# Positive scores in a queue of SBUF buffers, and value low parts on GpSimd from f32 copies

## The chip, the core and the metric

The kernel is written in Bass for one core of a Trainium2 chip. A core has a matrix engine (TensorE, PE in the profile; PEld its weight loads), three elementwise engines (VectorE = DVE, ScalarE = ACT, GpSimd = POOL), a sequencer that mainly issues transfers (SyncE = SP), an on-chip memory of 128 partitions (SBUF) and an accumulator memory of eight banks of 512 f32 columns (PSUM). Each engine runs its own queue in order; engines meet at semaphores that instructions count up and waits test. The metric is the device time of one execution in microseconds.

## What is computed

A trunk of two layers over 1024 tokens of width 1024. Layer 0 is stick-breaking and forgetting attention, layer 1 a sparse attention: an indexer scores all keys with 16 small heads, each query keeps its 256 best visible keys, and 16 heads attend over one shared latent. Each layer has a gated feed-forward with a causal convolution. The part of the reference that the change touches:

```python
idx_logits = jax.nn.relu(jnp.einsum('bqhd,bsd->bqhs', qib, kif))
score = jnp.einsum('bqh,bqhs->bqs', wb, idx_logits) * IDX_SCALE
score = jnp.where(visible[None], score, -jnp.inf)
top_val, top_idx = lax.top_k(score, topk)          # topk = 256
...
p = jax.nn.softmax(jnp.where(valid, logits, -jnp.inf), axis=-1)
ctx = einsum('bqhk,bqkc->bqhc', p, k_sel[..., DSA_ROPE:])
o = jnp.einsum('bshc,hcd->bshd', ctx, w_uv)        # per head; the kernel projects the latent first: values
```

## The kernel before, in words

Matrices are multiplied as bf16 pairs: every operand is split into a high part (the value cast to bf16) and a low part (the value minus its high part), and a product is three matmuls (high by high, low by high, high by low). The program is a list of phases. Each phase has a program for each engine, and an engine goes from one phase to the next with no barrier, held by semaphores alone.

**The index phase** (`index_sync`, `index_gpsimd`, `index_tensor`, `index_scalar`, `index_vector`). Eight strips `s` of index queries, two heads each. TensorE projects strip `s` in eight units of six matmuls (`strip_unit`, L1739) and, between the units, computes scores of strip `s - 2`: 12 score steps, one for each of two heads and six query blocks of 384 to 1024 columns (`scores`, L1783). Step t of a strip; a global number g counts them all. Step g writes the PSUM bank pair 0-1 or 2-3 in turn. ScalarE takes the relu of the pair in place (`relu`, L1837), VectorE multiplies it by the head's weight and adds it to `score` in SBUF (`add`, L1896; the first six, L1893, only multiply), and TensorE's step g waits for add g - 2 (the semaphore `s_ia`). The steps of strips 6 and 7 run beside two strips of the next product (`feed_q`).

For each strip ScalarE also copies the projection out of PSUM (`copy_strip`, L1811) and issues four DMAs that swap rows for the rotary embedding (L1816); GpSimd multiplies the swapped copy by the sine table (L1757) and splits one piece of weights (`split_piece`: `w_hi` L262, `w_lo` L265); VectorE multiplies by the cosine (L1865), adds the two (`rotate`, L1871) and later writes the low parts of the queries (`lows`, L1903), after ScalarE's high parts (`highs`, L1845). The order on ScalarE is: copy and DMAs of strip s, relus 0 to 4 of strip s - 1, highs of strip s, relus 5 to 11. On VectorE: cosine of s, adds 0 to 2, rotate, adds 3 to 6, lows, adds 7 to 11.

**The top-k phase** (`topk_*`). VectorE runs 32 rounds of `max` (L2106) and `match_replace` (L2110) over the six score blocks, then writes the additive mask `hide` (L2115 and small fills), and then the low parts of the attention values (`val_lo`, L2127). Meanwhile TensorE projects the 32 strips of queries (L292), ScalarE copies them out and makes high parts, GpSimd rotates and makes low parts (`q_out`, L2082). At its end TensorE projects the values in 16 chunks of 512 columns, one bank each (L2009): six matmuls a chunk. ScalarE writes the high part of a chunk (L2059), VectorE the low part from PSUM and the high part. Chunks 8 to 15 reuse banks and wait for `s_vl`, the count of low parts.

**Attention** (`attend_*`). TensorE waits for 12 low parts and computes the first latent scores (L2192), VectorE adds `hide` and takes the row maximum (L2270), ScalarE the exp (L2251), TensorE turns the result (L2228), and the product with the values follows (L2207). GpSimd copies the current heads' values (`v_now`, L2316) once all 16 low parts are there.

Elsewhere in the kernel VectorE normalises rows with L1255, a `scalar_tensor_tensor` whose two tensor operands are both in SBUF, while GpSimd splits weights.

## Time and profile before

| | us |
|---|---|
| median of 3 runs | 2972.35 (2971.84 to 2978.59) |
| profiled execution, device time | 2972.27 |
| its span in the trace | 2970.5 |
| PE busy | 2815.2 (95%) |
| DVE busy | 1890.6 (64%) |
| POOL busy | 1627.0 (55%) |
| ACT busy | 1082.4 (36%) |

In the trace the score steps run from about 1363 us of the span to 1546, the top-k rounds from there to 1877, the second half of the value chunks from 1883 to 1897, and attention from then on.

In a row of a timeline the first number is the start in microseconds of the span, the second the duration; a bracket at the end gives how long the engine stood idle before it and which instruction released it. Instructions of one engine overlap a little in these records, so the step from one start to the next is shorter than the duration (by about 0.08 us on VectorE). Matmul records are pipelined: what counts is the distance between their starts. A tile's name has its buffer number left out: `ps` is all of PSUM.

### The profile page before, as it was taken

To read this page: it belongs to the slowest core of one execution; us is meant where nothing else is said; L and a number is where in the kernel's file an instruction comes from. 1 tells how busy PE (TensorE), PEld (TensorE's weight loads), DVE (VectorE), ACT (ScalarE), POOL (GpSimd) and SP (SyncE) were. 2 spreads that over 40 slices of the span, in tenths; PEclk is the share of its full clock that TensorE was granted. 3 is DMA by queue.
4 is the path that set the end of the run, shared out by engine and by line. 5 is a ranking of instruction groups with operands and counts; after the bars stand their busy time and mean duration, and the time that the engine had idled before them with its cause. 6 is when DMAs were issued, how large, how long until landed. Compare 5 with 4: busy or idle time off the path is not lost.

```text
span 2970.5 us, 44602 instructions
## 1 busy us (share of the span) xinstructions
PE 2815.2 (95%) x16880; PEld 1459.1 (49%) x16880; DVE 1890.6 (64%) x2795; ACT 1082.4 (36%) x1781; POOL 1627.0 (55%) x867
## 2 busy tenths in 40 slices
PE   7999998899999999998789999799999999999998
PEld 3566655444444444443334444477764444444443
DVE  5777566485666674155679999777765856665042
ACT  3566676324333310014454333466650433332000
POOL 4777321456766778844238777300007566775884
PEclk9999999999999999999999999899999999999999
DMA  4122221431111143222103222111113211112422
GB/s 143 51 64 61 69 68 32 156 114 57 57 57 57 64 170 121 101 81 67 47 28 141 107 81 89 57 58 56 42 43 121 106 55 59 57 57 99 142 100 99
DMA packets 102988, 240.56 MB, mean 81 GB/s; under 512 B 42448, under 2 KB 42576, under 8 KB 102848
## 3 DMA queue, kind: packets, MB, share of 16 engines
q1 hardware_dynamic: 56352, 204.13, 19.2%
q10 hardware_dynamic: 46496, 34.48, 4.5%
q8 instruction: 97, 1.59, 0.2%
q14 instruction: 43, 0.35, 0.0%
HBM read 185.31 MB, written 31.51 MB: 73 GB/s over the span
## 4 chain that ended last, share of the span: by engine, by line
PE 70%; DVE 17%; issue 4%; ACT 4%; POOL 2%; ACTq 2%; DMA 0%; DVEq 0%; POOLq 0%
PE ps L1413 22%; PE ps L303 17%; PE ps L2192 6%; DVE best L2106 5%; DVE score L2110 5%; PE ps L553 5%; PE ps L327 4%; PE ps L292 3%; PE ps L2228 2%; PE ps L663 2%; PE ps L559 2%; PE ps L748 2%; PE ps L1739 1%; PE ps L2207 1%; PE ps L725 1%
## 5 line engine op out<-in xcount | busy, mean ns | idle before, releaser
L262 POOL TENSOR_TENSOR w_hi<-w_stage,ones 128x1024 bf16<-128x1024 f32 x147 | 303.9, 2067 | 342.7 <-PE ps L303 231.5
L265 POOL TENSOR_TENSOR w_lo<-w_stage,w_hi 128x1024 bf16<-128x1024 f32 x147 | 337.2, 2294 | 11.5
L1240 DVE SCALAR_TENSOR_TENSOR x_res<-x_res,ps 128x1024 f32<-128x1024 f32 x32 | 39.0, 1217 | 344.1 <-PE ps L303 344.1
L303 PE MATMUL ps<-w_hi,hid_hi 128*128 128x512 bf16 x704 | 209.6, 379 | 5.0 <-DVE x_res L1240 4.1
L303 PE MATMUL ps<-w_hi,hid_lo 128*128 128x512 bf16 x704 | 209.5, 379 | 0.0
L303 PE MATMUL ps<-w_lo,hid_hi 128*128 128x512 bf16 x704 | 209.4, 379 | 0.0
L2192 PE MATMUL ps<-lat_hi,q_now 128*128 128x512 bf16 (+3 forms) x768 | 197.7, 326 | 0.0
L1202 ACT ACTIVATE ln_rstd<-ln_rstd 128x1 f32<-128x1 f32 x32 | 6.5, 203 | 517.7 <-DVE ln_rstd L1249 517.7
L292 PE MATMUL ps<-xt_hi,w_hi 128*128 128x512 bf16 x608 | 180.9, 379 | 2.4 <-DVE score L1896 2.4
L292 PE MATMUL ps<-xt_lo,w_hi 128*128 128x512 bf16 x608 | 181.0, 379 | 0.0
L292 PE MATMUL ps<-xt_hi,w_lo 128*128 128x512 bf16 x608 | 180.9, 379 | 0.0
L2316 POOL COPY v_now_hi<-val_hi 128x512 bf16 (+1 forms) x16 | 9.8, 613 | 289.9 <-PE ps L2207 253.3
L2110 DVE MATCH_REPLACE8 score<-best,score 128x384 f32<-128x384 f32 (+2 forms) x192 | 165.8, 876 | 0.0
L1413 PE MATMUL ps<-xt_hi,w_lo 128*128 128x512 bf16 x432 | 163.8, 379 | 0.0
L1413 PE MATMUL ps<-xt_lo,w_hi 128*128 128x512 bf16 x432 | 163.8, 379 | 0.0
L1413 PE MATMUL ps<-xt_hi,w_hi 128*128 128x512 bf16 x432 | 163.8, 379 | 0.0
L2106 DVE MAX8 best<-score 128x8 f32<-128x384 f32 (+2 forms) x192 | 155.5, 879 | 3.3
L888 POOL TENSOR_TENSOR prob<-take,prob 128x1024 f32<-128x1024 f32 (+3 forms) x64 | 107.3, 1682 | 83.2 <-DVE prob L867 66.5
L1379 POOL TENSOR_TENSOR w_lo<-w_stage,w_hi 128x1024 bf16<-128x1024 f32 x36 | 76.6, 2128 | 113.6 <-ACT w_hi L1487 113.6
L684 DVE TENSOR_TENSOR pt_lo<-ps,pt_hi 128x512 bf16<-128x512 f32 x192 | 100.2, 549 | 56.4 <-ACT pt_hi L678 56.0
L663 PE MATMUL ps<-ident,prob 128*128 128x128 f32 x576 | 92.3, 287 | 41.6 <-DVE pt_lo L684 36.1
L2270 DVE CUSTOM_DVE_ANT_0 prob<-ps,hide 128x1024 f32<-128x1024 f32 (+7 forms) x128 | 96.5, 754 | 50.3 <-PE ps L2192 50.3
(284 smaller groups left out, 7721.5 us busy)
## 6 DMA issues: line engine op xcount, KB each, us to landing
w_stage<-in_l_up SPq DMA_DIRECT2D x88, 512.0 KB, 3.2
w_stage<-in_l_down SPq DMA_DIRECT2D x88, 512.0 KB, 3.2
w_stage<-in_l_o SPq DMA_DIRECT2D x32, 512.0 KB, 3.7
w_stage<-in_l_q SPq DMA_DIRECT2D x32, 512.0 KB, 4.8
q_split<-q_out SPq DMA_DIRECT2D x32, 512.0 KB, 2.6
q_now<-q_split SPq DMA_DIRECT2D x16, 1024.0 KB, 4.8
w_stage<-in_l_qkv SPq DMA_DIRECT2D x24, 512.0 KB, 3.3
x_spilled<-x_res ACTq DMA_DIRECT2D x16, 512.0 KB, 2.6
```

The costliest lines, as they stand in the source:

```text
L262: pool.tensor_tensor(w_hi[slot][:, 0:cols], w_stage[slot][:, 0:cols], ones[:, 0:1].to_broadcast([P, cols]), ALU.mult).then_inc(w_cast[slot ...
L265: pool.tensor_tensor(w_lo[slot][:, 0:cols], w_stage[slot][:, 0:cols], w_hi[slot][:, 0:cols], ALU.subtract).then_inc(w_split[slot], 1)
L292: mm = pe.matmul(ps[:, bank + h, :], w, a[:, k, h * HALF:(h + 1) * HALF], start=(first and k == k0 and m == 0), stop=(last and k == k1 - 1 ...
L303: mm = pe.matmul(ps[:, bank + h, :], a[:, k, rows], w[slot][:, h * HALF:(h + 1) * HALF], start=(k == 0 and m == 0), stop=(k == tiles - 1 a ...
L327: mm = pe.matmul(ps[:, bank + h, :], w, a[:, k, h * HALF:(h + 1) * HALF], start=(k == 0 and m == 0), stop=(k == KT - 1 and m == 2))
L553: mm = pe.matmul(ps[:, bank, :], w, a[:, u, h * HALF:(h + 1) * HALF], start=(u == 0 and m == 0), stop=(u == KT - 1 and m == 2))
L663: mm = pe.transpose(dst, self.prob[t % 4][:, cols], ident[:, :])
L888: pool.tensor_tensor(prob[t % 4][:, 0:n], take[t % 4][:, 0:n], prob[t % 4][:, 0:n], ALU.mult).then_inc(s_wsb, 1)
L1413: mm = pe.matmul(ps[:, bank, :], wk[:, k * P:(k + 1) * P], ak[:, k, :], start=(k == 0 and q == 0), stop=(k == 3 and q == 2))
L2106: dve.max(best[:, c, :], score[:, sc_at[i]:sc_at[i] + span[i]]).then_inc(s_top, 1)
L2110: dve.match_replace(cell, best[:, c, :], cell, TAKEN_SCORE).then_inc(s_rep, 1)
L2192: mm = pe.matmul(ps[:, 2 * (t % 2) + c // 512, 0:w], a, b, start=(kt == 0 and m == 0), stop=(kt == 1 and m == 2))
```

## The change

Index phase: the relu writes its result to one of four new f32 buffers in SBUF, `positive`, in turn, where it wrote back to PSUM. The add reads that buffer. TensorE's score step g now waits for relu g - 2 (`s_ir`) where it waited for add g - 2 (`s_ia`). Relu g waits for add g - 4, the last reader of its buffer.

Value chunks: ScalarE, after the high part, also copies the chunk in f32 to one of four new buffers, `val_f` (and waits, from the fifth on, for the low part four chunks back). The low part is made by GpSimd from `val_f` and the high part, behind all of its other work of the phase; VectorE's 16 subtractions are gone. TensorE's chunks 8 to 15 wait for the f32 copy (`s_vf`) where they waited for the low part. ScalarE waits for all 16 low parts ahead of attention.

```diff
--- before.py
+++ after.py
@@ -1699,6 +1699,7 @@
         ki_hi, ki_lo = [room(n, [P, SEQ], BF16) for n in ("ki_hi", "ki_lo")]
         strip_f = [room(f"strip_f{b}", [P, SEQ], F32) for b in range(2)]
         strip_w = [room(f"strip_w{b}", [P, SEQ], F32) for b in range(2)]
+        positive = [room(f"positive{b}", [P, SEQ], F32) for b in range(4)]
 
         s_tl5 = sem("tables_loaded")
         s_f5, s_c5, s_s5, s_a5, s_h5, s_l5 = [sem(n) for n in
@@ -1776,7 +1777,7 @@
                 if g % IDX_STEPS == 0:
                     pe.wait_ge(s_l5, strip_lows(s))
                 if g >= 2:
-                    pe.wait_ge(s_ia, g - 1)
+                    pe.wait_ge(s_ir, g - 1)
                 for c in range(0, span[i], 512):
                     w = min(512, span[i] - c)
                     for m, keys in enumerate((ki_hi, ki_lo)):
@@ -1834,7 +1835,9 @@
             def relu(g):
                 s, hh, i, bank = idx_step(g)
                 act.wait_ge(s_iq, g + 1)
-                act.activation(banks(bank)[:, 0:span[i]], banks(bank)[:, 0:span[i]], ACT.Relu).then_inc(s_ir, 1)
+                if g >= 4:
+                    act.wait_ge(s_ia, g - 3)
+                act.activation(positive[g % 4][:, 0:span[i]], banks(bank)[:, 0:span[i]], ACT.Relu).then_inc(s_ir, 1)
 
             def highs(s):
                 act.wait_ge(s_a5, 2 + s + 1)
@@ -1886,7 +1889,7 @@
 
             def add(g):
                 s, hh, i, bank = idx_step(g)
-                cell, src = score[:, sc_at[i]:sc_at[i] + span[i]], banks(bank)[:, 0:span[i]]
+                cell, src = score[:, sc_at[i]:sc_at[i] + span[i]], positive[g % 4][:, 0:span[i]]
                 w = w_idx[:, i, 2 * s + hh:2 * s + hh + 1]
                 dve.wait_ge(s_ir, g + 1)
                 if g < len(picky):
@@ -1929,6 +1932,7 @@
         after_qs = room.at
         q_out = [room(f"q_out{b}", [P, 2, SEQ], BF16) for b in range(4)]
         best = room("best", [P, len(picky), 8], F32)
+        val_f = [room(f"val_f{b}", [P, HALF], F32) for b in range(4)]
         s_cp, s_cw6, s_co, s_si, s_ro, s_qh, s_ql = [sem(n) for n in
             ("q_copied", "q_swapped", "q_cos", "q_sin", "q_rotated", "q_hi_written", "q_lo_written")]
         assert room.at <= q_now_at
@@ -1941,6 +1945,7 @@
         val_hi, val_lo = [val_room(n, [P, TB, N_DSA, 64], BF16) for n in ("val_hi", "val_lo")]
         assert val_room.at <= after_qs
         s_val, s_vh, s_vl = sem("values_projected"), sem("values_hi_written"), sem("values_lo_written")
+        s_vf = sem("values_copied")
         VAL_CHUNKS = 2 * TB
 
         def chunk_bank(c):
@@ -2001,7 +2006,7 @@
                 if c < 8:
                     pe.wait_ge(s_cp, 4 * (feed_q.iters - 1) + c // 2 + 1)
                 else:
-                    pe.wait_ge(s_vl, (c + Q_BANK[0]) % 8 + 1)
+                    pe.wait_ge(s_vf, (c + Q_BANK[0]) % 8 + 1)
                 for n in range(2):
                     slot = feed_uv.slot(n)
                     cols = slice(half * HALF, (half + 1) * HALF)
@@ -2057,6 +2062,9 @@
                 hi, _, src = value_views(c)
                 value_done(act, c)
                 act.activation(hi, src, ACT.Copy).then_inc(s_vh, 1)
+                if c >= 4:
+                    act.wait_ge(s_vl, c - 3)
+                act.activation(val_f[c % 4][:, :], src, ACT.Copy).then_inc(s_vf, 1)
 
         def topk_gpsimd(pool):
             def split(r, i):
@@ -2092,6 +2100,11 @@
                                    ALU.subtract).then_inc(w_split[slot], 1)
 
             over_strips(pool, split, finish, split_values)
+            for c in range(VAL_CHUNKS):
+                hi, lo, _ = value_views(c)
+                pool.wait_ge(s_vh, c + 1)
+                pool.wait_ge(s_vf, c + 1)
+                pool.tensor_tensor(lo, val_f[c % 4][:, :], hi, ALU.subtract).then_inc(s_vl, 1)
 
         def topk_vector(dve):
             dve.wait_ge(s_ia, IDX_STEPS * KT)
@@ -2121,10 +2134,6 @@
                 if i not in picky:
                     end = at_of[i] + span[i]
                     dve.memset(hide[0:CHUNK, end - CHUNK:end], MASKED).then_inc(s_hide, 1)
-            for c in range(VAL_CHUNKS):
-                hi, lo, src = value_views(c)
-                dve.wait_ge(s_vh, c + 1)
-                dve.tensor_tensor(lo, src, hi, ALU.subtract).then_inc(s_vl, 1)
 
 
 
@@ -2329,6 +2338,7 @@
             all_latent_pairs(pe, latent_tensor)
 
         def attend_scalar(act):
+            act.wait_ge(s_vl, VAL_CHUNKS)
             for r in range(4):
                 act.wait_ge(s_qst[r], 16 * feed_q.iters)
             all_latent_pairs(act, latent_scalar)
```

## Rows read from the trace of the kernel before

**Rows 1.** The page's chain that ended last: shares of the span by engine, line.

```profile
PE 70%; DVE 17%; issue 4%; ACT 4%; POOL 2%; ACTq 2%; DMA 0%; DVEq 0%; POOLq 0%
PE ps L1413 22%; PE ps L303 17%; PE ps L2192 6%; DVE best L2106 5%; DVE score L2110 5%; PE ps L553 5%; PE ps L327 4%; PE ps L292 3%; PE ps L2228 2%; PE ps L663 2%; PE ps L559 2%; PE ps L748 2%; PE ps L1739 1%; PE ps L2207 1%; PE ps L725 1%
```

**Rows 2.** Stretches: length, busy us of PE, PEld, DVE, ACT, POOL; clock, DMA.

```profile
1380.85:1404.28 23.43, 18.51 (x89) 7.88 (x88) 15.76 (x17) 11.68 (x15) 6.33 (x3) 1.00 0.16 45
1404.28:1428.29 24.01, 18.51 (x89) 7.87 (x88) 15.75 (x17) 11.68 (x15) 6.33 (x3) 1.00 0.17 44
1475.14:1500.58 25.44, 20.06 (x90) 8.22 (x88) 15.86 (x17) 11.68 (x15) 6.32 (x3) 0.93 0.15 42
```

**Rows 3.** PE timeline: start, us, what, [idle before it <- what ended it].

```profile
1371.55 0.39 PE L1783 MATMUL ps<-ki_hi,qi 128*128 128x512 bf16 x1 [1.87 <-DVE score L1893]
1388.49 0.39 PE L1783 MATMUL ps<-ki_hi,qi 128*128 128x512 bf16 x1 [2.24 <-DVE score L1896]
```

**Rows 4.** Timeline of ACT: the strip copy and its DMA issues (ACTq).

```profile
1383.77 1.02 ACT L1811 ACTIVATE strip_f<-ps 128x1024 f32<-128x1024 f32 x1
1384.82 2.44 ACTq L1816 DMA_DIRECT2D strip_w<-strip_f  x4
```

**Rows 5.** Timelines of POOL and DVE, same strip: sine, split, an add.

```profile
1389.03 2.35 POOL L1757 TENSOR_TENSOR strip_w<-strip_w,rope_i_sin 128x1024 f32<-128x1024 f32 x1 [15.73 <-DMA strip_w<-strip_f]
1391.33 1.89 POOL L262 TENSOR_TENSOR w_hi<-w_stage,ones 128x1024 bf16<-128x1024 f32 x1
...
1392.62 1.01 DVE L1896 SCALAR_TENSOR_TENSOR score<-ps,w_idx,score 128x768 f32<-128x768 f32 x1
```

**Rows 6.** Adds L1896 (ns min/median/max); the group of the lows (mean ns).

```profile
L1896 DVE SCALAR_TENSOR_TENSOR score<-ps,w_idx,score x90: 607/946/1285, 1374.9 to 1544.9; 128x384 f32<-128x384 f32 x15, 128x512 f32<-128x512 f32 x15, 128x640 f32<-128x640 f32 x15, 128x768 f32<-128x768 f32 x15
...
L1903 DVE TENSOR_TENSOR qi<-ps,qi 64x1024 bf16<-64x1024 f32 x16 | 19.5, 1222 | 1.6 <-ACT qi L1845 1.1
```

**Rows 7.** L1255 (ns min/median/max), then timelines of DVE and POOL.

```profile
L1255 DVE SCALAR_TENSOR_TENSOR x_res<-x_res,ln_mv,g_rows_o x16: 1276/2909/3016, 593.8 to 2332.3; 128x1024 f32<-128x1024 f32 x16
...
593.76 2.98 DVE L1255 SCALAR_TENSOR_TENSOR x_res<-x_res,ln_mv,g_rows_o 128x1024 f32<-128x1024 f32 x1
...
593.77 1.89 POOL L262 TENSOR_TENSOR w_hi<-w_stage,ones 128x1024 bf16<-128x1024 f32 x1 [3.50 <-PE ps L303]
595.74 2.98 POOL L265 TENSOR_TENSOR w_lo<-w_stage,w_hi 128x1024 bf16<-128x1024 f32 x1
```

**Rows 8.** Stretches of the value product: first half, second half, the gap.

```profile
1857.07:1867.43 10.36, 10.36 (x49) 4.61 (x47) 10.15 (x20) 6.14 (x10) 4.24 (x2) 1.00 0.59 216
1883.44:1896.62 13.18, 13.18 (x48) 5.42 (x49) 6.35 (x10) 4.18 (x7) 0.00 (x0) 0.78 0.00 1
1867.43:1883.44 16.01, 0.17 (x2) 0.01 (x1) 15.70 (x34) 0.60 (x1) 0.00 (x0) 0.65 0.14 58
```

**Rows 9.** Timeline of DVE: hide writes; the first masked maximum of attention.

```profile
1877.61 2.70 DVE L2115 TENSOR_SCALAR hide<-score 128x384 bf16<-128x384 f32 x6
...
1899.63 1.23 DVE L2270 CUSTOM_DVE_ANT_0 prob<-ps,hide 128x1024 f32<-128x1024 f32 x1 [1.49 <-PE ps L2192]
```

**Rows 10.** Timeline of ACT: values' high parts; table load ahead of exp.

```profile
1861.63 2.72 ACT L2059 ACTIVATE val_hi<-ps 128x512 bf16<-128x512 f32 x5 [2.24 <-POOL q_out L2082]
...
1901.15 1.28 ACT L2251 ACT_TABLE_LOAD   x1 [3.73 <-DVE neg_max L2274]
```

**Rows 11.** POOL by shape: count, busy us, mean ns, idle before; two sizes.

```profile
L2082 POOL TENSOR_TENSOR q_out<-qs_f,q_out 128x1024 bf16<-128x1024 f32 x32 | 68.2, 2133 | 19.2 <-ACT q_out L2045 19.2
...
L265 POOL TENSOR_TENSOR w_lo<-w_stage,w_hi 128x128 bf16<-128x128 f32 x1 | 0.4, 425 | 0.1
```

**Rows 12.** DVE by shape, around the value product: the largest hide write.

```profile
L2115 DVE TENSOR_SCALAR hide<-score 128x1024 bf16<-128x1024 f32 x1 | 0.7, 686 | 0.0
```

**Rows 13.** Casts L484 (ns min/median/max); POOL's timeline at the slow one.

```profile
L484 DVE CAST gate_p<-gate_c x3: 681/681/2267, 34.5 to 39.3; 8x1024 bf16<-8x1024 f32 x3
...
38.29 2.76 POOL L876 TENSOR_TENSOR w_hi<-w_stage,ones 128x1024 bf16<-128x1024 f32 x1 [8.17 <-PE ps L553]
```

## Prediction, made before the changed kernel was run

> **What bounds the kernel now.** I read first the chain that ended last [rows 1]: TensorE holds 70% of the span and VectorE 17%, nearly all of the latter the top-k rounds (L2106, L2110, 10% together). So the span is TensorE's work, plus the top-k, plus the places where TensorE stands still. The change touches two such places.
>
> The first is the index stage. The table by stretches [rows 2] cuts it at the start of score step 10 of each strip: six strips take 23.43 us (four of them), 24.01 and 25.44 us, together 143.2 us. A matmul of 512 columns takes 10.36 / 48 = 0.216 us [rows 8]; a strip has 8 units of 6 (1.295 each) and 12 score steps of as many columns as 33 matmuls (7.1), 17.5 us with no stall. The rows of TensorE give the cause: its score matmuls wait for VectorE's add (L1896) [rows 3], and by the code adds wait for relus and relus for score matmuls. One step must go through three engines before its bank pair is free, and there are two pairs. So a strip of 23.43 stands still for 5.9 us in all; the longest stall is before score step 2, 2.24 us of idle time [rows 3], and that one is not the add's own doing: ScalarE's queue has the strip copy and four DMA issues (1383.77 to 1387.26 [rows 4]) between relu 11 and relu 0.
>
> The second is the end of the value product. TensorE has done eight chunks at 1867.43 and stands still for 16 us [rows 8], because banks are given back by `val_lo`, which is queued on VectorE behind the last top-k round and the `hide` writes (to 1880.3) [rows 9]. The other eight chunks then take 13.18 us against 10.36 for the first eight: the granted clock was 0.78 there and 1.00 before, so both levels, 1.2 and 2.4 GHz, are in that stretch.
>
> **The change, index stage.** What goes: TensorE's wait for add g-2. What comes: a wait for relu g-2 on TensorE, and on ScalarE a wait for add g-4 before relu g. Queued behind that ScalarE wait are the strip copy, its four swap DMAs and the `qi` highs. No instruction is added. The relu now writes SBUF; the strip copy writes SBUF too and takes 1.02 us for 1024 columns [rows 4], and the same gap between instructions, so I take the relu's price as unchanged (per strip it could be 0.3 us either way before anyone waits).
>
> I lay one strip out with durations of the trace, zero at score step 10. Steps 10, 11, unit 0, step 0, unit 1 and step 1 run to 4.96 without a stall. Relus 10 and 11 end at 1.83 and 2.86, the copy at 3.90, its DMA issues at 6.38 (2.44 of them), relu 0 at 6.90 [rows 4]. Step 2 starts at 6.95 (before: 7.64), a stall of 2.0 us that stays. From there to step 6 nothing waits. The swaps land 1.77 us after the last issue, GpSimd's sine takes 2.35 [rows 5], `rotate`, of the lows' size, 1.23 [rows 6]: ready at 11.8, while relu 4 ends at 12.6, so the highs (2.05) aren't delayed, relu 5 ends at 15.7 and step 7 waits 0.45. Next step 10: 20.0. That is the strip with VectorE free.
>
> It isn't free. The add used to read one operand from PSUM; now it reads two from SBUF, and that form has a row: L1255, same operation and size, 1.276 us at its shortest, 2.9 median, and 2.98 where GpSimd's weight split (1.89) began with it; the next GpSimd operation then took 2.98 for its 2.13 [rows 7]. The present add, with one operand in PSUM, ran at its usual 1.01 (768 columns) inside a GpSimd split [rows 5]. So the new form and GpSimd take turns, whole instruction by whole instruction, and the price of the new add without GpSimd is the old one (1.276 against at most 1.285 [rows 6]).
>
> The Trainium skill (SBUF — State Buffer, Who interferes with whom) states this against the change: a VectorE instruction with two SBUF inputs and a GpSimd instruction that reads SBUF block each other wholly, and by issue order alone. By that rule the sum is the one below; had I priced the add by its old rows alone, the strip would be the 20.0 above, and the total 3 us less.
>
> Per strip GpSimd has three operations (2.35 + 1.89 + 2.13 [rows 5, 7]). VectorE's own work is 12 adds of 0.946, each overlapping the next by 0.08 (10.4), and cosine, rotate and two lows of 1.22 [rows 6], likewise (4.7): 15.1 us. With turns: add 2 (ready 8.4) waits for the sine until 10.5, ends 11.4; rotate isn't held, 12.6; add 3 waits for `w_hi` until 13.3; add 4 for `w_lo` until 16.3; add 5 ends 18.6, add 6 19.1, lows 21.5, add 7 22.2. Relu 11 of the next strip needs add 7 and would be due at 21.9, so it and the copy come 0.4 late; the lows end just as TensorE wants to begin the next strip (21.6). I take 20.5 us a strip. Bounds: 20.0 if no turn is taken, 22 if the held adds cost 1.5 us more (VectorE then sets the pace, with nothing to hide it).
>
> Six strips: 143.2 - 6 x 20.5 = 20.2 us. Two strips were long for other reasons (the ScalarE issues of one, the clock at 0.93 in the other [rows 2]), together 2.6 us; I leave half of it in the new kernel: 18.9. The strip before (scores of strip 0) has a stall of 1.87 us on an add behind `rotate` [rows 3] and a second of about a microsecond behind the lows, which go: 2.8. The last two rounds, with no strip copy behind the first, have no such stall, and the last add still ends before the top-k. **Index: 21.7 us** (12 to 26). The top-k loop is VectorE's alone and moves earlier unchanged.
>
> **The change, values.** Removed: 16 subtractions on VectorE. Added: 16 copies on ScalarE, 16 subtractions on GpSimd, ScalarE's wait for low c-4 in each, and ScalarE's wait for all lows ahead of attention. TensorE now gets a bank back at the copy. ScalarE starts at 1861.6 (after GpSimd's last `q_out`, as before [rows 10]) and needs 0.53 + 0.53 a chunk: chunk 4 is copied at 1867.1, just before TensorE wants its bank at 1867.4, and later ones keep ahead (1.06 against 1.295). So TensorE runs 16 chunks on end at 10.36 per eight and is done at 1857.07 + 20.72 = 1877.8, with no slow clock.
>
> A GpSimd low of 128x512 has no row; the same operation takes 2.13 at 1024 columns and 0.425 at 128 [rows 11], so 1.15 by the line between them (bounds: half of 2.13, and 0.425 x 4 = 1.70; I take 1.15, since 1024 columns cost 5 times 128, not 8). First at 1862.8, the twelfth, which lets attention's first scores begin, at 1876.7: not late. Three are left when VectorE comes to `hide` (1877.6). Those `hide` writes are 0.686 us for 1024 columns [rows 12], half of what VectorE needs for that size elsewhere (1.276 [rows 7]): a double-rate form. Another form at that rate, the cast L484 with a single SBUF input, took 0.681 twice and 2.267 under a GpSimd operation [rows 13]. So I expect the six `hide` writes and the last lows to take turns: 2.7 + 3 x 1.15 + the rest of the one in progress, `hide` done at 1884.0 in place of 1880.3, lows at about 1882.3.
>
> The first masked maximum then starts at 1884.05; before it started at 1899.63 [rows 9]. That is 15.6 us, and TensorE has two score blocks done by then, which gives about 0.2. If `hide` isn't held, TensorE's scores set it: 1877.8 + 3.0 = 1880.8, or 18.8 us. ScalarE's exp waits for the maximum (table load at 1901.15 before [rows 10]), not for the lows, in both. GpSimd's `v_now` copies follow the lows and move earlier by as much as attention does. At 1.70 a low, six lows are still to come and every `hide` write waits for one: 1877.6 + 2.7 + 6 x 1.70 = 1890.5, 9 us gained. **Values: 15.8 us** (9 to 18.8).
>
> **Sum.** 21.7 + 15.8 = 37.5 us from the profiled run of 2972.27 (span 2970.5, 1.8 around it), 2934.8; it is as good as the median, 2972.35. Forecast **2935**, its own range 2926 to 2944.
>
> **Rivals.** (1) The port eats the index gain: VectorE sets the pace at 22 to 23 us. For: lows and add 7 end with no slack in my strip. Against: GpSimd works 6.4 us of 20. Index 10, total 26: 2946. (2) The ring doesn't free TensorE: relu g is held by add g-4, and ScalarE's copy and DMAs with it, until the old 23.9 returns. For: VectorE is busy 15.1 of 20 with 4 us of waits to come. Against: four buffers against two. Index 0 to 3, total 17: 2955. (3) GpSimd's lows take much longer than 1.15 beside the top-k and gate attention through ScalarE's new wait: at 2.1 each the sixteenth ends 1896.4; total 21.7 + 4.8: 2946. Against: `q_out` runs at 2.13 under the same top-k rounds. (4) Slower: the loop copy, DMA issue, landing, sine, rotate, adds 3 to 6, lows, add 7, relu 11, copy closes on itself through the ring, 21 us with the turns I counted. It costs time only if each strip exceeds 23.86 + 18.6/6 = 27.0 us, that is if the holds come to 6 us more, as much as all of GpSimd's work again; at 28.5 the total is 2981.
>
> **How the numbers follow.** Forecast 0.68, (1) 0.13, (2) 0.07, (3) 0.05, (4) 0.04, within 0.3% (8.9 us, about what a measurement of this kernel tells from no change) by a mix of (2) and (3) 0.03. The range takes in the forecast's, (1) and (3), and leaves (2), (4) out: 2925 to 2951. Faster by over 0.3%: 0.93; within: 0.03; slower: 0.04.
>
> **What would show it.** Right: strips of about 20.5 us; adds of 128x1024 still near 1.28 but some near 3; GpSimd splits near 3 in the index stage; one stall of 2 us at step 2; no gap in the value product, the granted clock 1.00 there; `hide` writes over 1 us each; first masked maximum about 7 us after the last top-k instruction (before 22). Wrong: strips over 22 us with relus waiting for adds; ScalarE's first exp released by GpSimd.

## The result, and the profile after

The changed kernel takes 2932.24 us, median of four runs (2928.89 to 2936.75), beside 2972.1 us for the kernel before on the same chip (2964.36 to 2978.59): ratio 0.9864, 95% interval 0.9848 to 0.988, 40 us less. Two later series of it, each beside the kernel before on its chip, gave 2934.99 us (ratio 0.9883, 0.9867 to 0.99) and 2931.84 us (0.9864, 0.9848 to 0.9881). The profiled execution took 2930.87 us, span 2929.1.

The page of the changed kernel, its line of busy time (share of the span, instructions). TensorE is busy 96% of it:

```profile
PE 2804.3 (96%) x16880; PEld 1457.9 (50%) x16880; DVE 1905.8 (65%) x2779; ACT 1089.6 (37%) x1797; POOL 1652.5 (56%) x883
```

The spans differ by 41.4 us (2970.5 and 2929.1). The two stages account for 36.3 of them; another 6.4 us is there already when TensorE starts on strip 2 (1355.25 us against 1361.62), and it is there before the first line of the change runs: the first L1240 starts at 575.37 us, before at 582.18. It belongs to the execution, not to the change, for in two later profiled executions of the changed kernel (2932.07 and 2931.14 us) that line starts at 582.60 and 581.23. Behind the second head of attention 1.3 us go the other way.

**The index stage: 25.0 us less.** From TensorE's start on strip 2 to the first top-k instruction there were 185.24 us, and there are 160.2 (1355.25 to 1515.45). The table by stretches of the changed kernel, cut at score step 10 of each strip as in [rows 2], and the strip before them last:

```profile
1374.01:1393.84 19.83, 17.86 (x90) 8.27 (x89) 18.22 (x16) 11.59 (x15) 7.51 (x3) 1.00 0.19 53
1393.84:1413.70 19.86, 17.88 (x90) 8.26 (x89) 19.51 (x17) 11.60 (x15) 7.50 (x3) 1.00 0.20 54
...
1473.19:1493.05 19.86, 17.89 (x90) 8.26 (x89) 19.52 (x17) 11.59 (x15) 7.50 (x3) 1.00 0.20 54
1355.25:1374.01 18.76, 17.75 (x81) 8.04 (x82) 13.10 (x12) 8.96 (x12) 6.63 (x3) 0.91 0.29 85
```

All six strips take 19.83 to 19.86 us, where they took 23.43 to 25.44. VectorE looks full, 19.5 us of 19.86. The same instructions took 15.76 before [rows 2]; the 3.7 us more are instructions drawn out beside GpSimd's. TensorE's timeline shows the two waits left in a strip, at score step 2 and at step 7, both ended by a relu:

```profile
1420.59 0.39 PE L1784 MATMUL ps<-ki_hi,qi 128*128 128x512 bf16 x1 [1.80 <-ACT positive L1840]
1429.30 0.39 PE L1784 MATMUL ps<-ki_hi,qi 128*128 128x512 bf16 x1 [0.23 <-ACT positive L1840]
```

Behind the first stand ScalarE's strip copy and four DMA issues (compare [rows 4]). The timelines of ACT, POOL and DVE in the same strip:

```profile
1416.44 1.02 ACT L1812 ACTIVATE strip_f<-ps 128x1024 f32<-128x1024 f32 x1
1417.49 2.45 ACTq L1817 DMA_DIRECT2D strip_w<-strip_f  x4
...
1421.72 2.35 POOL L1758 TENSOR_TENSOR strip_w<-strip_w,rope_i_sin 128x1024 f32<-128x1024 f32 x1 [12.26 <-DMA strip_w<-strip_f]
1424.03 2.47 POOL L262 TENSOR_TENSOR w_hi<-w_stage,ones 128x1024 bf16<-128x1024 f32 x1
1426.58 2.72 POOL L265 TENSOR_TENSOR w_lo<-w_stage,w_hi 128x1024 bf16<-128x1024 f32 x1
...
1422.08 2.67 DVE L1899 SCALAR_TENSOR_TENSOR score<-positive,w_idx,score 128x640 f32<-128x640 f32 x1 [0.22 <-ACT positive L1840]
```

The add of 640 columns starts while the sine runs and takes 2.67 us (before, this size took 879 ns in the mean); the two splits take 2.47 and 2.72, not 1.89 and 2.13 [rows 5, 7]. Grouped by shape, the adds of the whole stage (line, engine, count, busy us, mean ns):

```profile
L1899 DVE SCALAR_TENSOR_TENSOR score<-positive,w_idx,score 128x896 f32<-128x896 f32 x15 | 28.4, 1892 | 2.3 <-ACT positive L1840 2.3
L1899 DVE SCALAR_TENSOR_TENSOR score<-positive,w_idx,score 128x640 f32<-128x640 f32 x15 | 24.0, 1597 | 1.4 <-ACT positive L1840 1.4
L1899 DVE SCALAR_TENSOR_TENSOR score<-positive,w_idx,score 128x1024 f32<-128x1024 f32 x15 | 19.1, 1276 | 0.0
```

128x1024, which never meets GpSimd, costs 1276 ns as it did with PSUM (1285 at most, [rows 6]); 640 and 896 columns are the ones held most (879 and 1151 ns before), 768 in part (1211 ns, before 1015).

**The values: 11.3 us less in this execution, 14.4 and 14.3 us in two others.** The measure is the time from VectorE's first instruction behind the top-k (the memset of `hide`) to the masked maximum that begins the second head. Of the kernel before, VectorE's timeline:

```profile
1877.20 0.37 DVE L2118 MEMSET hide<- 128x64 uint32 x2
...
1918.03 1.22 DVE L2270 CUSTOM_DVE_ANT_0 prob<-ps,hide 128x1024 f32<-128x1024 f32 x1 [1.55 <-PE ps L2192]
```

That is 40.83 us. Of the changed kernel, the timelines of VectorE, GpSimd, TensorE and ScalarE:

```profile
1845.78 0.37 DVE L2131 MEMSET hide<- 128x64 uint32 x2
1846.19 9.05 DVE L2128 TENSOR_SCALAR hide<-score 128x384 bf16<-128x384 f32 x6
...
1855.52 1.22 DVE L2279 CUSTOM_DVE_ANT_0 prob<-ps,hide 128x1024 f32<-128x1024 f32 x1
...
1875.33 1.23 DVE L2279 CUSTOM_DVE_ANT_0 prob<-ps,hide 128x1024 f32<-128x1024 f32 x1 [1.55 <-PE ps L2201]
...
1831.43 17.90 POOL L2107 TENSOR_TENSOR val_lo<-val_f,val_hi 128x512 bf16<-128x512 f32 x16 [1.26 <-ACT val_f L2067]
1849.40 0.62 POOL L2325 COPY v_now_hi<-val_hi 128x512 bf16<-128x512 bf16 x1
...
1852.43 2.26 POOL L262 TENSOR_TENSOR w_hi<-w_stage,ones 128x1024 bf16<-128x1024 f32 x1
...
1856.81 0.61 PE L2201 MATMUL ps<-lat_hi,q_now 128*128 128x512 bf16 x1 [5.41 <-DVE row_max L2279]
...
1857.04 1.28 ACT L2260 ACT_TABLE_LOAD   x1 [9.38 <-DVE neg_max L2283]
```

From memset to second head: 29.55 us. The 16 us gap of TensorE [rows 8] is gone; in its place is one wait of 5.41 us, for the masked maximum, behind six `hide` writes that take 9.05 us. By shape, the first and the last of these writes:

```profile
L2128 DVE TENSOR_SCALAR hide<-score 128x384 bf16<-128x384 f32 x1 | 3.4, 3359 | 0.0
L2128 DVE TENSOR_SCALAR hide<-score 128x1024 bf16<-128x1024 f32 x1 | 2.4, 2376 | 0.0
```

The first stood until 1849.55, when the last of the 16 lows was done (1831.43 + 17.90 = 1849.33); the last, 0.69 us of work [rows 12], until 1855.25, right after the weight split (1854.69). In a second profiled execution of the same kernel the same view reads:

```profile
L2128 DVE TENSOR_SCALAR hide<-score 128x384 bf16<-128x384 f32 x1 | 1.2, 1185 | 0.0
...
L2128 DVE TENSOR_SCALAR hide<-score 128x1024 bf16<-128x1024 f32 x1 | 1.1, 1092 | 0.0
```

There VectorE got in between the lows, the last write was issued before the weight split, and the six took 6.69 us; memset to second head 26.47 us (1852.62 to 1879.09). A third execution gave 6.75 and 26.54.

### The profile page after: what moved, and what is told of

Same layout as the page of the kernel before. It is cut to its first block and busy times, and to the rows that moved or that the text cites. A ratio compares the mean times of both kernels' runs of the same rounds, so it can differ in the third digit from the quotient of the medians.

```text
span 2929.1 us, 44727 instructions
## 1 busy us (share of the span) xinstructions
PE 2804.3 (96%) x16880; PEld 1457.9 (50%) x16880; DVE 1905.8 (65%) x2779; ACT 1089.6 (37%) x1797; POOL 1652.5 (56%) x883
## 5 line engine op out<-in xcount | busy, mean ns | idle before, releaser
L1240 DVE SCALAR_TENSOR_TENSOR x_res<-x_res,ps 128x1024 f32<-128x1024 f32 x32 | 38.9, 1217 | 343.2 <-PE ps L303 343.2
```

## The experiments

The theory: the gain is two separate ones, each a bank pair given back to TensorE earlier; VectorE's adds and `hide` writes now take turns with GpSimd, at no cost to the strips and at a cost of some us at the top-k's end. The first four kernels ran beside a kernel before of 2973.84 us (2969.88 to 2976.86).

**Each part alone.** The kernel before with one half of the change:

```
 index alone:                                    values alone:
-  pe.wait_ge(s_ia, g - 1)                      -  pe.wait_ge(s_vl, (c + Q_BANK[0]) % 8 + 1)
+  pe.wait_ge(s_ir, g - 1)                      +  pe.wait_ge(s_vf, (c + Q_BANK[0]) % 8 + 1)
 (and the ring of positive)                      (and val_f, GpSimd's lows, ScalarE's waits)
```

> Only the index part of the change (relu into four SBUF buffers, TensorE waits for the relu); the values stay as before. My theory from the two traces: the index stage, from the first score step to the first top-k round, is 25 us shorter by itself and nothing later gives it back, so 24 to 26 us under the kernel before, strips at 19.8 us. Rival: the parts need each other (the earlier index end is only worth its time with the value part behind it): then the index part alone gives under 20 us.

> Only the value part (f32 copies, low parts on GpSimd). Theory: 11 to 12 us under the kernel before, with the hide writes at about 9 us in place of 2.7, as in the changed kernel. With e1 the two add up to 36 us, and the other 4 to 6 us between the two profiled executions are no part of the change. Rival: the change's gain is 40 us and the parts overlap or help each other, so that e1 and e2 add up to 40 or more.

Index alone: 2947.74 us, ratio 0.991 (0.9894 to 0.9927), 26.1 us less. Values alone: 2962.6 us, ratio 0.9964 (0.9952 to 0.9977), 11.2 us less. Together 37.3 us, against 36.7 to 40 for both at once: they add up, neither gives back the other's gain. In the profile of the first the strips take 19.84 to 19.87 us from copy to copy and the `hide` writes their 2.70 us of before. In the second the value stage by itself shows 14.5 us, not 11.2 (VectorE's timeline):

```profile
1878.10 0.37 DVE L2128 MEMSET hide<- 128x64 uint32 x2
1878.50 7.20 DVE L2125 TENSOR_SCALAR hide<-score 128x384 bf16<-128x384 f32 x6
...
1904.38 1.22 DVE L2276 CUSTOM_DVE_ANT_0 prob<-ps,hide 128x1024 f32<-128x1024 f32 x1 [1.54 <-PE ps L2198]
```

26.28 us from memset to second head, 14.5 under 40.83; the total's interval, 6.8 to 14.3 us, only just leaves this out. In this execution the index stage, whose code is the old one, is the longer: from ScalarE's copy of the second strip to the top-k 189.9 us against 186.7 in the kernel before, with two strips at a granted clock of 0.93. That takes 3.2 of the 14.5 us back. What no run separates is the two parts of the value change: the copies alone, with the lows left on VectorE, were not measured.

**A ring of two buffers.** Is it the depth of the ring that frees TensorE?

```
-        positive = [... for b in range(4)]
+        positive = [... for b in range(2)]
-                if g >= 4:
-                    act.wait_ge(s_ia, g - 3)
+                if g >= 2:
+                    act.wait_ge(s_ia, g - 1)
 ...                                             (and positive[g % 2] in relu and add)
```

> The changed kernel with two positive buffers in place of four; relu g waits for add g - 2. Theory: VectorE comes about 2.8 us late with add 7 (it stands behind the low parts), and four buffers hide that; with two, relu 9 waits for it, and a strip takes 22 to 23.4 us in place of 19.8: most of the index gain is gone, the total is 15 to 22 us above the changed kernel. Rival (it is enough that TensorE no longer waits for the add itself, the depth of the queue does not matter): strips stay under 20.5 us, total within 4 us of the changed kernel.

2948.62 us, ratio 0.9917 (0.9899 to 0.9935): 16.4 us over the changed kernel's first median, within the 15 to 22 expected, and 10 to 16 by the ratios of its three series. The strips take 21.8 us, a little under the 22 to 23.4 expected. ScalarE's timeline shows a relu held by an add, and TensorE's what that makes of it:

```profile
1419.24 0.49 ACT L1840 ACTIVATE positive<-ps 128x384 f32<-128x384 f32 x1 [1.13 <-DVE score L1899]
...
1419.79 0.39 PE L1784 MATMUL ps<-ki_hi,qi 128*128 128x512 bf16 x1 [1.02 <-ACT positive L1840]
```

From ScalarE's copy of the second strip to the top-k it takes 172.0 us; the changed kernel takes 161.7, the kernel before 186.7. So two buffers give 15 of the 25 us, and the other two are worth 10, or 12 beside the kernel with the copies held (below), whose index code is the changed kernel's and which takes 159.6 us there, with no stretch of low clock. The two profiled executions differ by 16 us, since this one is also 8.2 us later at that copy (1361.96 against 1353.75), before the ring could matter, and 3.5 us shorter from memset to second head. The number was hit, its working only for two thirds; why the medians are 16 us apart stays open. This goes part of the way of rival (2).

**What the turns cost the strips.** Now GpSimd splits only 8 columns of each weight while the strips run:

```
-                    split_piece(pool, feed_qidx, s, 1)
+                    split_little(pool, feed_qidx, s, 1)      # 8 columns
```

> This kernel leaves work out: in the loop over the strips of the index stage GpSimd splits only 8 of each weight's columns into high and low parts, so the other columns of those weights stay unsplit. It tells what the turns with VectorE cost in time. Theory: the adds are held by GpSimd's splits, but VectorE has enough idle time to take that, and the strip's length is set by ScalarE's strip copy and DMA issues and by TensorE. Then adds 3 to 6 lose their holds (the stretch from add 3 to add 6 falls by about 2 us and more), and the strips stay at 19.8 us within 0.1; total within 2 us of the changed kernel. Rival (the port is part of the path): strips of 19.4 us or less, total 2.5 us or more shorter. The sine stays, so the second add is still held by it.

2931.89 us, ratio 0.9876 (0.9859 to 0.9893), beside 2934.99 us for the changed kernel in the same series: 3.1 us less, where at most 2 was expected, with intervals that overlap (0.9867 to 0.99). The profiled executions differ in a stretch ahead of the third copy: 20.52 us from the second to the third copy at a granted clock of 1.00, 22.64 at 0.92 in the changed kernel's; most of that 2.1 us is not the splits' work, for the kernel with the copies held (below) has whole splits and takes 20.91 at 1.00. The strips stay at 19.82 to 19.84 us. VectorE's adds 3 and 4 together and TensorE's stalls, in the same strip:

```profile
1429.59 2.06 DVE L1909 SCALAR_TENSOR_TENSOR score<-positive,w_idx,score 128x768 f32<-128x768 f32 x2
...
1424.36 0.39 PE L1794 MATMUL ps<-ki_hi,qi 128*128 128x512 bf16 x1 [1.75 <-ACT positive L1850]
...
1433.08 0.39 PE L1794 MATMUL ps<-ki_hi,qi 128*128 128x512 bf16 x1 [0.22 <-ACT positive L1850]
```

Two adds in 2.06 us: no hold is left there, and TensorE stands still exactly as long as before. So the turns with the splits cost the strips nothing. What is left to set 19.83 us is, by the stall at step 2, ScalarE's copy with its four issues.

**Take those issues away.** SyncE issues the swaps from the third strip on, and the loads of the next product's weights, which it used to issue beside them, behind each strip's swaps. Another kernel holds GpSimd's `v_now` copies too (see below).

```
-                    act.dma_start(strip_w[b][to:to + 32, :], strip_f[b][a:a + 32, :])...
+                if m < 2:
+                    swap_strip(act, m, b, heads, rotated)
 (index_sync)
-            load_first(sp, feed_q)
+            for s in range(KT):
+                swap_strip(sp, 2 + s, s % 2, 2, s + 1)
+                if 1 <= s <= 4:
+                    load_piece(sp, feed_q, s - 1, 0)
```

> The changed kernel, but the four swap DMAs of each strip from the third on are issued by SyncE, not by ScalarE behind its strip copy. Theory: the stall of 1.75 us before score step 2 is ScalarE's (copy and four DMA issues between relu 11 and relu 0); without the issues relu 0 runs about 2.4 us earlier and that stall goes, while the swaps land about as before, and the highs then make TensorE wait up to 1.6 us at step 7. Strips of 18.1 to 19.2 us, six rounds 4 to 9 us shorter, total 4 to 8 us under the changed kernel. Rival (another wait lies right behind, an add held by the sine or the highs): strips stay at 19.6 us or more, and the total changes by less than 2 us.

> The changed kernel again, beside the others on the same chip, as the measure of what they gain. Expected: 1.36% under the kernel before, 40 us, within 4 us; strips of 19.8 us and hide writes of about 9 us in all.

2935.75 us (0.9882, 0.9866 to 0.9899) beside the changed kernel's 2934.99: no gain, the rival was right. One strip took 19.2 us, the next three are back at 19.83, and the one after them takes 21.29 at a granted clock of 0.92. Its timelines of ACT, SyncE's queue, POOL and PE in one strip:

```profile
1418.16 1.02 ACT L1847 ACTIVATE positive<-ps 128x1024 f32<-128x1024 f32 x1 [0.16 <-DVE score L1906]
1419.09 1.02 ACT L1822 ACTIVATE strip_f<-ps 128x1024 f32<-128x1024 f32 x1
...
1428.57 2.06 ACT L1855 ACTIVATE qi<-ps 64x1024 bf16<-64x1024 f32 x2 [1.82 <-DVE ps L1881]
...
1420.13 2.41 SPq L1750 DMA_DIRECT2D strip_w<-strip_f  x4
...
1424.37 2.35 POOL L1768 TENSOR_TENSOR strip_w<-strip_w,rope_i_sin 128x1024 f32<-128x1024 f32 x1 [12.26 <-DMA strip_w<-strip_f]
...
1431.73 0.39 PE L1794 MATMUL ps<-ki_hi,qi 128*128 128x512 bf16 x1 [2.16 <-ACT positive L1847]
```

The stall at step 2 is gone, and step 7 stands still 2.16 us instead, since the highs wait 1.82 us for `rotate`. And relu 11 is now released by an add: the loop of rival (4), copy, issue, landing, sine, rotate, adds 3 to 6, lows, add 7, relu 11, copy, has closed. Its length is what the strips show, 19.83 us. I had summed it at 21.

**Both at once.** If that loop binds now, the turns, which cost nothing above, must cost something here:

> The kernel with SyncE's swaps, and GpSimd splitting only 8 of each weight's columns in the loop over the strips (the other columns stay unsplit, that work is left out). It tells what holds the strips at 19.83 us once ScalarE no longer issues the swaps. Theory: a loop through the ring of buffers, copy, swap, sine, rotate, adds 3 to 6 (6.2 us with GpSimd's turns in them), lows, add 7, relu 11, copy; without the turns the adds 3 to 6 take about 3.8 us, relu 11 is no longer released by an add, and what is left is the loop through the highs: step 7 comes 12.64 us after the copy began, and the next copy 6.98 us after step 7 (as in the changed kernel), 19.6 us; so strips of 19.5 to 19.7 us. Rival (GpSimd's turns have nothing to do with it): strips of 19.8 us, relu 11 still released by an add.

Relu 11 is no longer held, and the strips fall to 19.07 to 19.12 us, under even the 19.5 to 19.7 expected (total 2928.42, one run). VectorE's and TensorE's timelines:

```profile
1423.55 1.23 DVE L1891 TENSOR_TENSOR ps<-ps,strip_w 128x1024 f32<-128x1024 f32 x1 [2.39 <-POOL strip_w L1778]
1424.69 2.07 DVE L1916 SCALAR_TENSOR_TENSOR score<-positive,w_idx,score 128x768 f32<-128x768 f32 x2
...
1427.98 0.39 PE L1804 MATMUL ps<-ki_hi,qi 128*128 128x512 bf16 x1 [1.45 <-ACT positive L1857]
```

`rotate` starts 7.72 us after the copy (1415.83), with only the sine before it; with SyncE's swaps and whole splits it was 8.23. So the same splits are free beside one bound and cost 0.75 us a strip beside the next. It holds the other way round too: with the small splits, ScalarE's issues are the difference between 19.83 (above) and 19.08 us. Each alone gives nothing, both together 0.75, and that shows two bounds of the same length. My 19.6 had left `rotate` where it was; these 0.5 us are what it missed.

**Halve the issues instead.** ScalarE issues two swaps, SyncE the other two:

```
+                swap_strip(act, m, b, 0, 64 * heads if m < 2 else 64, rotated)
+                swap_strip(sp, 2 + s, s % 2, 64, 128, s + 1)
 ...                                             (and the weight loads behind them, as above)
```

> The changed kernel with the four swap DMAs of each strip from the third on issued by two engines: ScalarE two behind its copy, SyncE the other two at the same time. Theory: two waits of nearly the same length bind the strip, ScalarE's copy and four issues ahead of relu 0, and the loop from the copy over the landing, sine, rotate, adds and lows to add 7 and relu 11. The kernel with SyncE's swaps took the first away and fell on the second, of the same 19.84 us. Two issues fewer ahead of each, about 1.2 us, shorten both: the stall at step 2 falls from 1.75 to 0.6 us, the sine starts 1.2 us earlier after the copy, and strips take 18.5 to 18.9 us; six strips 5.5 to 8 us less, total 4 to 8 us under the changed kernel. Rival (something else binds, the holds of the adds or the highs): strips of 19.5 us or more.

> The changed kernel again, beside the two with two queues on the same chip. Expected 1.2 to 1.4% under the kernel before; strips of 19.83 us; hide writes between 6.5 and 11 us in all, differing from one execution to the next.

2933.95 us beside 2931.84: no gain. Strips of 19.43 once, then 20.04, 20.04, 19.84, 19.83. The stall at step 2 did shrink, to 0.84 us, but step 7 waits 1.35, and the sine came no sooner after the copy, 5.56 us against 5.28. Timelines of ACT, SyncE's queue and POOL (its second row is two strips later), and the DMA part of the first stretch (issues: count, KB each, median us to landing):

```profile
1420.20 1.02 ACT L1822 ACTIVATE strip_f<-ps 128x1024 f32<-128x1024 f32 x1
1421.25 1.41 ACTq L1750 DMA_DIRECT2D strip_w<-strip_f  x2
...
1421.25 1.14 SPq L1750 DMA_DIRECT2D strip_w<-strip_f  x2
...
1425.76 2.86 POOL L1768 TENSOR_TENSOR strip_w<-strip_w,rope_i_sin 128x1024 f32<-128x1024 f32 x1 [12.53 <-DMA strip_w<-strip_f]
...
1465.04 2.67 POOL L1768 TENSOR_TENSOR strip_w<-strip_w,rope_i_sin 128x1024 f32<-128x1024 f32 x1 [11.93 <-DMA strip_w<-strip_f]
...
strip_w<-strip_f SPq DMA_DIRECT2D x2, 128.0 KB, 2.6
strip_w<-strip_f ACTq DMA_DIRECT2D x2, 128.0 KB, 3.4
```

The issues end 1.0 and 1.3 us earlier after the copy, but landing takes 2.6 and 3.4 us where it took 2.3 (page of either kernel). The load of 512 KB that goes out right behind is a small part of this: in the two strips copied at 1440.24 and 1460.08 us no load follows, and landing still takes 2.6 or 2.7 and 3.1 us. So most of it comes with the two queues; why, no run here shows. I had counted the issue and not the transfer. And a sine that comes sooner gains nothing. In the strip copied at 1460.08 it starts 4.96 us after the copy, 0.3 earlier than in the changed kernel, but an add is running: it takes 2.67 us for 2.35, `rotate` starts 8.23 us after the copy as in the changed kernel (8.23), and relu 11 is again released by an add. Where the load follows, the sine takes 2.86 to 3.02 us and `rotate` starts at 8.52.

**GpSimd's copies held until `hide` is done.**

```
             pool.wait_ge(s_vl, VAL_CHUNKS)
+            pool.wait_ge(s_hide, 2 * TB - len(picky))
             for hh in range(2):
                 values_now(hh, 0)
```

> The changed kernel, with GpSimd held until the hide writes are done before it copies the current values and splits the first output weights. Theory (hide writes and GpSimd operations take turns): only the last three low parts still hold the hide writes, so they take about 6 us in place of 9.05, TensorE's wait before its third score block shrinks from 5.4 to about 2.5 us and its matmuls after it stay at 0.216 us apart (2.4 GHz level): 3 to 5.5 us faster than the changed kernel, about 2928. Rival (the hide writes are slow for another reason, such as ScalarE's or TensorE's traffic): they stay at about 9 us and the time stays at 2932, or rises because the copies come late.

> Both: the swap DMAs issued by SyncE, and GpSimd's copies of the values held until the hide writes are done. Theory: the hold is worth about 4 us from the last top-k instruction to the attention of the second head, as its profile showed (25.6 us in place of 29.6), and its median was no lower because runs spread by some 4 us; with the swaps' 4 to 8 us the total is 7 to 11 us under the changed kernel. Rival (the 4 us are given back behind the second head, where GpSimd's copies or the weight splits are late): as the kernel with SyncE's swaps alone, within 1.5 us.

> The kernel with the swaps on two queues, and GpSimd's copies of the values held until the hide writes are done. Theory: how the hide writes and GpSimd fall together differs from one execution to the next (9.05 us and 6.69 us in two executions of the same kernel), so the hold is worth 1 to 4 us: hide writes of 5.7 to 6.7 us, 25.3 to 26 us from the last top-k instruction to the attention of the second head, total 0 to 4 us under the kernel with two queues alone. Rival: no difference, or slower.

In the first of these kernels the `hide` writes fall to 5.71 us, as expected. By shape, its first and its last write, and the second largest of the second kernel:

```profile
L2128 DVE TENSOR_SCALAR hide<-score 128x384 bf16<-128x384 f32 x1 | 3.4, 3372 | 0.0
...
L2128 DVE TENSOR_SCALAR hide<-score 128x1024 bf16<-128x1024 f32 x1 | 0.7, 680 | 0.0
...
L2135 DVE TENSOR_SCALAR hide<-score 128x896 bf16<-128x896 f32 x1 | 1.6, 1572 | 0.0
```

Only the first write is held there, by three lows; the others cost their bare time (680 ns, [rows 12]). In the other two kernels with the hold the six take 6.67 and 6.86 us, no less than the changed kernel's 6.69 and 6.75: four of them, of 1.37 to 1.58 us, take turns with the lows. So there are two patterns. Where the first write stands behind three or more lows, the copies and the split meet the rest, and the hold takes 9.05 down to 5.71 us; where lows and writes alternate from the start, it takes nothing off the writes.

From memset to second head the three kernels with the hold show 25.58, 25.75 and 25.95 us; the changed kernel's three executions 29.55, 26.47 and 26.54, and other kernels without the hold 26.0 to 31.1. So the hold is worth 4 us there in the first pattern and 0.5 to 0.8 us in the second. The first kernel's own expectation of matmuls that stay at the higher level failed. Stretches from the first masked maximum to the second head's (columns as in [rows 2]), of the changed kernel and of this one:

```profile
1855.52:1875.33 19.81, 18.30 (x182) 12.90 (x182) 12.47 (x34) 12.36 (x27) 13.66 (x7) 0.84 0.12 35
...
1856.09:1875.27 19.18, 17.39 (x180) 12.72 (x183) 12.56 (x34) 12.44 (x27) 18.23 (x12) 0.91 0.11 36
```

TensorE's wait fell from 5.41 to 2.30 us, but the granted clock is still 0.91, and 0.8 us of 19.18 is lost beside the 18.40 at clock 1.00. The totals hardly tell the hold: 2932.66 us (0.9869, 0.9853 to 0.9886), where 3 to 5.5 us under the changed kernel was expected; 2934.6 beside 2934.99, where 7 to 11 us less was expected; 2930.08 (0.9855, 0.9838 to 0.9872) beside 2933.95 without the hold and 2931.84 for the changed kernel. The last has the lowest median of the kernels that do all the work, and its interval overlaps the changed kernel's: no version here is shown to beat it.

## Why the prediction was right, point by point

The forecast was 2935 us, 37.5 us under the profiled run; the first measurement is 2932.24, and three comparisons give 36.7 to 40 us. The two terms by themselves:

- **Index, 21.7 us predicted, 25.0 in the profile** (26.1 alone). The mechanism held: step 2 starts 6.88 us after step 10 (6.95 predicted), with 1.75 to 1.80 us of stall (2.0). Adds 3 to 6 were laid out at 6.5 us with the turns and take 6.17; add 2 was to wait for the sine, and does. What failed is the last sentence of that layout, that add 7 would be late for relu 11 and the copy, which made 20.5 of 20.0. Add 7 ends 1.73 us into the next strip, relu 11 is due at 1.85. The turns are hidden whole, as the kernel with small splits shows. The strip is 0.17 under my own bound with VectorE free, since the stalls at steps 2 and 7 (0.23, not 0.45) are shorter. Six strips: 24.2 us, where 18.9 was entered.
- **The odd strips.** I left 1.3 us for them among the six and 2.8 us of gain in the strip before. The six have none. All that lies around them gained only 25.0 - 24.2 = 0.8: the strip before has the granted clock at 0.91, both levels in it (2.4 and 1.2 GHz), after TensorE had stood still 2.25 us. From 1356.55 to 1360.07 us its matmuls of 512 columns are 0.43 us apart, instead of 0.216, which costs 1.8 us. The other two executions of the changed kernel have such a stretch in the same strip (granted clock 0.92 and 0.93 between its copies); the kernel with the copies held has the same stall, 2.26 us, and a clock of 1.00, so the stall alone doesn't decide it.
- **Values, 15.8 us predicted, 11.3 in the first profile, 14.4 and 14.3 in the others.** The value product runs without a gap at clock 1.00. The lows were entered at 1.15 us and come 1.12 apart; the port's turns were expected, and the six writes with them at 6.4 us. They took 9.05, 6.69 and 6.75. The step that failed is the sentence on the `v_now` copies, which had them only "follow the lows and move earlier": they and the first weight split come upon `hide` and take their turns too. The kernel with the copies held shows it for the first of these executions (5.71, with three lows ahead of the first write in both); in the other two the sum of 6.4 us was nearly right. The count of turns, three lows in all, held in the first profile, but there all three fell on the first write.
- **Behind `hide`** I gave back 0.2 us for the scores already done. Instead from the first masked maximum to the second head's it takes 19.81 us (18.40 before): TensorE has stood still 5.41 us, and the granted clock of this stretch is 0.84. Where it stood still 3.23 us (the other two executions) the stretch took 19.1 at 0.91; where it stood still 2.12 us (values alone) 18.40 at 1.00. This 1.4 us had no term in the sum.
- **The rivals.** (1), VectorE setting the pace, and (2), the ring not freeing TensorE, did not come; a ring of two goes part of the way of (2). (3), slow lows, did not: 1.12 us. (4) was named with the right members and a length of 21 us, and it does exist, at 19.83, as soon as ScalarE's issues are out of the way; it never came near the 27 us at which it costs time.

The two errors, 3.3 us too little for the index and 1.5 to 4.5 too much for the values, nearly cancel. That the total came within 3 us of the forecast is in part luck. The mechanism held, and each term stayed within its own bounds (12 to 26 and 9 to 18.8 us).

The Trainium skill (SBUF — State Buffer, Who interferes with whom), on which the turns leaned beside the rows, says who issues first has the shared ports for the whole instruction. The adds and splits agree (2.67 us for 0.88, 2.47 for 1.89); that a write arriving during one low came in after three, and in another execution of the same kernel after one, is not decided by that sentence, and no run here shows what decides it.

## What to carry to other kernels

When a step is moved to another engine, count every instruction queued behind it there, for these move as well and meet new neighbours: here the lows were counted, and the copies and the weight split behind them were not, which in one execution of three took the `hide` writes from 5.7 to 9.05 us. Before removing the wait that binds, lay out the next loops with their lengths; where they lie close together (here 19.83 through ScalarE's issues, 19.84 through the ring, and an estimated 19.6 through the highs, measured at 19.1 without the splits), taking one away gives nothing, and a cost that was free can become real. A stall on TensorE can also cost what the lower clock takes afterwards: here 1.4 us behind one of 5.41, 0.7 to 0.8 behind 2.30 and 3.23, nothing behind 2.12.

## What the runs showed of the hardware that was not expected

- Turns between VectorE and GpSimd don't alternate strictly: the first `hide` write of 0.35 us or so took 3.36 us behind three lows in one execution and 1.19 in another, of the same program; the six together 6.69 to 9.05 us, and 10.78 in the kernel with SyncE's swaps, whose first write took 5.09.
- GpSimd's plain copies take part too: `v_now` copies of 512 bf16 columns take 0.61 us by themselves and up to 0.93 beside the `hide` writes in one execution, 1.07 in another.
- The multiply (`add` of the first six steps) with one f32 operand in SBUF and f32 output took 0.75 us for 1024 columns, 1.28 with that operand in PSUM in the kernel before: the same double rate that the `hide` writes have.
- Splitting four DMA issues over two queues ended the issue 1.0 to 1.3 us earlier and lengthened the landing from 2.3 us to 2.6 and 3.1, and to 3.4 with a load of 512 KB issued right behind them.
